# Stick-breaking attention in a four-layer trunk: the two newest key blocks' softplus values added once on VectorE, so that one matmul sums both

## The chip, the cores and the metric

The program runs on one core of a Trainium2 chip. The metric is the device time of one execution in microseconds; below 2% (some 57 us here) a difference counts as no difference in the verdicts.

## What is computed

A trunk of four layers is evaluated for 512 prompt frames and 64 sample frames, with D = 1024. Layers 0 and 3 mix with stick-breaking attention (16 heads of 64), layer 1 with a short gated convolution, layer 2 with gated linear attention; a squared-ReLU MLP follows each. Only the attention is touched:

```python
def stick_breaking_block(q, k, v, q_pos, k_pos):
    z = einsum('bqhd,bkhd->bhqk', q, k) * (SB_HEAD_DIM ** -0.5)
    mask = k_pos[None, :] < q_pos[:, None]
    log_not = where(mask, log_sigmoid(-z), 0.0)
    rev = cumsum(log_not, axis=3, reverse=True)
    tail = pad(rev[..., 1:], ...)
    a = where(mask, exp(log_sigmoid(z) + tail), 0.0)
    return einsum('bhqk,bkhd->bqhd', a, v)
```

So the weight of a key needs, beside its own score, the sum of softplus(z) = -log_sigmoid(-z) over all keys that are newer than it. The prompt's queries attend to the prompt's keys, the 64 sample queries to 256 cached keys and their own 64.

## The kernel before

Everything lies in SBUF: activations X as 8 blocks of 128 rows by 576 tokens (512 prompt, 64 sample). Dense layers run in slabs of 256 weight columns. SyncE loads a slab into `raw[:, s % 2]`; ScalarE rounds it to a high part `whi` (L766), VectorE makes the low part `wlo` (L1096); TensorE multiplies with three products for each 128x128 block (L384: high by high, high by low, low by high), always in two halves of 288 tokens. That is most of the time. The order on every engine is the order in which the code is written; the engines meet only in counting semaphores.

The attention of a layer is eight head pairs (`PAIRS`), each of three units, so 24 units u. A unit is one block of 128 key rows against all queries that see it, for both heads e = 0, 1. `b = 2 - u % 3`:

- u % 3 == 0 (b = 2), 448 columns: key block 2 against query blocks 2 and 3 (columns 0 to 255), key block 3 against query block 3 (256 to 383), the sample's own 64 keys (384 to 447).
- u % 3 == 1 (b = 1), 512 columns: key block 1 against query blocks 1 to 3 (0 to 383), cached keys 0 to 127 (384 to 447) and 128 to 255 (448 to 511) against the sample.
- u % 3 == 2 (b = 0), 512 columns: key block 0 against all four query blocks.

For a unit, `scores` (L441, L448) puts masked scores into one of three PSUM pairs `zduo[u % 3]`. ScalarE takes Exp (L867) and Ln (L872) of them into `weighted(u)`; VectorE's `softplus` clamps the result (L1201), rounds it to a high part (L1205, signals `sp_hi`) and subtracts for the low part (L1207, signals `sp_lo`), both in `parts(u)`. Then `cumulative(u)` on TensorE (L474, signals `r_ready`) adds the sums over newer keys to the scores in PSUM: for each part and each e, a triangular matmul over the unit's own columns and then matmuls with a matrix of minus ones, one for each newer key block and query range. ScalarE's `weights(u)` (L877, signals `a_ready`) takes Exp of the total over `weighted(u)`, and `weighted_values(u)` (L505) multiplies by the values. `scores(u)` waits for `weights(u - 3)`, since they use the same PSUM pair.

TensorE's order in the steady loop is `scores(k + 2)`, `cumulative(k)`, `weighted_values(k - 1)`; ScalarE's is `weights(k - 1)`, `logs(k + 1)`, `exponents(k + 2)`; VectorE runs `softplus(u)` one after the other, with `output` after u % 3 == 1. The first units are woven into a head in which cached keys and values are transposed on TensorE (L526, L534) and copied out by VectorE (L1175) and ScalarE (L840).

`split_r` is the same memory as the `raw` slabs: its upper half (`raw[:, 1]`) serves as `parts(u)` for u % 4 == 3. SyncE loads the output projection's slab 1 into it once three units from the last are summed (`r_ready`, `units - 3`). The lower half, `raw[:, 0]`, takes slab 2 directly behind it.

Of the kernel before, what the change touches and what calls it, by code (L numbers as in the profile page):

```python
# [82 lines left out]
def trunk(nc, x_prompt, x_sample, cache_sb_k, cache_sb_v, state_conv, state_gla, norm_mix, norm_mlp, sb_w_qkv, sb_w_o,  # L83
          conv_w_in, conv_w, conv_w_out, gla_w_in, gla_w_gk2, gla_b_gk, gla_norm, gla_w_o, mlp_w_up, mlp_w_down,
          norm_final, y_prompt, y_sample, sb_k_p, sb_v_p, sb_k_s, sb_v_s, conv_p, conv_s, gla_p, gla_s):
    with ExitStack() as ctx:
# [76 lines left out]
        ck_in, cv_in = sem("ck_in"), sem("cv_in")  # L163
        z_ready, e_ready, l_ready, sp_ready = (sem(n) for n in ("z_ready", "e_ready", "l_ready", "sp_ready"))
        sp_hi, sp_lo, r_ready, a_ready, av_done = (sem(n) for n in ("sp_hi", "sp_lo", "r_ready", "a_ready", "av_done"))
        sbt_ready, sbt_v, sbt_a = sem("sbt_ready"), sem("sbt_v"), sem("sbt_a")

        u_ready, y_ready, g_ready, conv_pre = sem("u_ready"), sem("y_ready"), sem("g_ready"), sem("conv_pre")
# [53 lines left out]
        def parts(u):  # L222
# [9 lines left out]
                return [v.rearrange("p (e c) -> p e c", e=2) for v in (hi, lo)]  # L232
            return [both[:, i * D:(i + 1) * D].rearrange("p (e c) -> p e c", e=2) for i in range(2)]

        zduo = [duo[i][:, :].rearrange("p (e c) -> p e c", e=2) for i in range(3)]
        obank, osbank = bank[6], bank[7]

# [81 lines left out]
        @block.sync  # L319
        def _(sp):  # L320
            for t in range(NT):
                src = x_prompt[0, t * P:(t + 1) * P, :] if t < 4 else x_sample[0]
                n = P if t < 4 else TS
                sp.dma_start(flat(0, 9)[0:n, t * D:(t + 1) * D], src).then_inc(x_in[t], 16)

            def load(base, w, count, units=None):
                def body(s, u):
                    sp.wait_ge(w_lo, base + s + 1)
                    if units is not None and isinstance(s, int) and s == 1:
                        sp.wait_ge(r_ready, units - 3)  # L330
                    sp.dma_start(raw[:, u], w[:, :, bass.ds(s * SLAB, SLAB)]).then_inc(slab_in[u], 16)
                slabs(sp, count, body, 0 if units is None else 2)

            for layer in range(4):
                base = first_slab(layer)
                if layer == 2:
                    for i, of in enumerate((0, 2 * D, D)):
                        load(base + OUT_SLABS * i, mix_in[layer][:, :, of:of + D], OUT_SLABS)
                elif layer == 1:
                    for s in range(IN_SLABS):  # L340
                        col = P * in_chunk(layer, s, 0)
                        sp.wait_ge(w_lo, base + s + 1)
                        sp.dma_start(raw[:, s % 2], mix_in[layer][:, :, col:col + SLAB]).then_inc(slab_in[s % 2], 16)
                else:
                    load(base, mix_in[layer], IN_SLABS)
                load(base + IN_SLABS, mix_out[layer], OUT_SLABS, UNITS * (layer // 3 + 1) if layer in (0, 3) else None)
                for g in range(GROUPS):
                    b = base + IN_SLABS + OUT_SLABS + 2 * OUT_SLABS * g
                    load(b, cols(mlp_w_up[layer][:, g * D:(g + 1) * D]), OUT_SLABS)
                    load(b + OUT_SLABS, cols(mlp_w_down[layer][g * D:(g + 1) * D, :]), OUT_SLABS)  # L350


            for t in range(NT):
                dst, n = (y_prompt[0, t * P:(t + 1) * P, :], P) if t < 4 else (y_sample[0], TS)
                sp.wait_ge(y_v, t + 2)
                sp.wait_ge(y_a, t + 1)
                sp.dma_start(dst, VT[0:n, t, :]).then_inc(y_stored, 16)
            sp.wait_ge(y_stored, 16 * NT)
            sp.wait_ge(kv_stored, 16 * 8)
            sp.wait_ge(stored, 16 * STORES)  # L360
# [3 lines left out]
        def _(pe):  # L364
# [64 lines left out]
            def stick_breaking(layer, sb_index):  # L429
# [36 lines left out]

                def cumulative(u):

                    b, z = 2 - u % 3, zduo[u % 3]
                    for part, ready in ((0, sp_hi), (1, sp_lo)):  # L470
                        pe.wait_ge(ready, first + u + 1)
                        for e in range(2):
                            def acc(which, lo, hi, back, of):
                                return pe.matmul(z[:, e, lo:hi], sums[:, which, :], parts(u - back)[part][:, e, of:of + hi - lo],  # L474
                                                 start=False, stop=False, skip_group_check=True)
                            mm = acc(0, 0, WIDE[u % 3], 0, 0)
                            if b == 2:
                                mm = acc(1, 128, 256, 0, 256)
                            elif b == 1:
                                acc(1, 128, 384, 1, 0)  # L480
                                acc(1, 256, 384, 1, 256)
                                acc(1, 384, 448, 1, 384)
                                acc(1, 448, 512, 1, 384)
                                mm = acc(1, 384, 448, 0, 448)
                            elif b == 0:
                                acc(1, 128, 512, 1, 0)
                                acc(1, 256, 512, 2, 0)
                                mm = acc(1, 384, 512, 2, 256)
                    mm.then_inc(r_ready, 1)

                def weighted_values(u):
# [267 lines left out]
        def _(act):  # L759
# [97 lines left out]
            def stick_breaking(layer, sb_index):  # L857
                first = UNITS * sb_index

                def exponents(u):  # L860
                    if u == 0 and sb_index:
                        act.wait_ge(kv_stored, 16 * 4 * sb_index)
                    if u >= 5:
                        act.wait_ge(av_done, first + u - 4)
                    act.wait_ge(z_ready, first + u + 1)
                    w = WIDE[u % 3]
                    act.activation(weighted(u)[:, :, 0:w], zduo[u % 3][:, :, 0:w], ACT.Exp).then_inc(e_ready, 1)  # L867

                def logs(u):
                    e = weighted(u)[:, :, 0:WIDE[u % 3]]  # L870
                    act.wait_ge(e_ready, first + u + 1)
                    act.activation(e, e, ACT.Ln, bias=1.0).then_inc(l_ready, 1)  # L872

                def weights(u):
                    w = WIDE[u % 3]
                    act.wait_ge(r_ready, first + u + 1)
                    act.activation(weighted(u)[:, :, 0:w], zduo[u % 3][:, :, 0:w], ACT.Exp).then_inc(a_ready, 1)  # L877

                def output(p):
                    act.wait_ge(av_done, first + 3 * p + 3)  # L880
                    act.activation(hhi[:, p, 0:TP], obank[:, :], ACT.Copy)
                    act.activation(hhi[:, p, TP:T], osbank[:, 0:TS], ACT.Copy).then_inc(mix_hi, 1)

                def cached_keys(n):
                    sb_evacuate(sb_index, n, CKT[:, 2 * n:2 * n + 2, :].rearrange("p c k -> p (c k)"), bank[7][:, :])

                exponents(0)
                cached_keys(1)
                logs(0)
                exponents(1)  # L890
                cached_keys(3)
                logs(1)
                values(sb_index, 5)
                exponents(2)
                values(sb_index, 7)
                weights(0)
                values(sb_index, 9)
                logs(2)
                values(sb_index, 11)
                values(sb_index, 13)  # L900
                exponents(3)
                for k in range(2, UNITS + 1):
                    weights(k - 1)
                    if k % 3 == 1:
                        output((k - 4) // 3)
                    if k + 1 < UNITS:
                        logs(k + 1)
                    if k + 2 < UNITS:
                        exponents(k + 2)
                output(PAIRS - 1)  # L910
# [178 lines left out]
        def _(dve):  # L1089
# [102 lines left out]
            def stick_breaking(layer, sb_index):  # L1192
                first = UNITS * sb_index

                def softplus(u):

                    w = WIDE[u % 3]
                    s = weighted(u)[:, :, 0:w]
                    hi, lo = (t[:, :, 0:w] for t in parts(u))
                    dve.wait_ge(l_ready, first + u + 1)  # L1200
                    dve.scalar_tensor_tensor(s, s, LN_MAX, zduo[u % 3][:, :, 0:w], ALU.min, ALU.max).then_inc(sp_ready, 1)  # L1201
                    dve.wait_ge(sp_ready, first + u + 1)
                    if u >= 4:
                        dve.wait_ge(r_ready, first + last_sum(u - 4) + 1)
                    dve.tensor_copy(hi, s).then_inc(sp_hi, 1)  # L1205
                    dve.wait_ge(sp_hi, first + u + 1)
                    dve.tensor_tensor(lo, s, hi.bitcast(F32), ALU.subtract).then_inc(sp_lo, 1)  # L1207

                def output(p):
                    dve.wait_ge(mix_hi, 8 * layer + p + 1)  # L1210
# [556 lines left out]
```

## Time and profile before

| | us |
|---|---|
| runs | 2845.40, 2875.87, 2877.62 |
| median of the runs | 2875.87 |
| profiled execution, own time | 2865.92 |
| its span | 2864.2 |
| TensorE busy in it | 2822.2 (99%) |
| VectorE busy | 1257.0 (44%) |
| ScalarE busy | 862.1 (30%) |
| mean granted TensorE clock | 0.993 of full |

The span is the profiled part of an execution; its own time is 1.7 us more. A busy share tells how long an engine had something in flight, not that it was at its peak: a matmul's row lasts longer than the distance to the next one's start. The attention of layer 0 stands from about 175 to 307 us, that of layer 3 from about 2250 to 2382 us.

### The profile page before, as it was taken

How to read it: one execution, taken by the hardware profiler on the slowest of the kernel's cores; microseconds unless marked ns; L12 is line 12 of the kernel's file. 1: busy time of each engine (PE TensorE's matmuls, PEld its weight loads, DVE VectorE, ACT ScalarE, POOL GpSimd, SP SyncE). 2: the span in 40 equal slices, each digit the busy share in tenths (PEclk: the TensorE clock that was granted, in tenths of full speed). 3: DMA queues.
4: the chain of work that ended last, by engine and by line, in shares of the span. 5: the costliest groups of instructions: out<-in, count | busy, mean ns of one | idle time of the engine just before them, and what ended most of it. 6: DMA issues, size and time to landing. Idle time of an engine off the chain costs nothing.

```text
span 2864.2 us, 49238 instructions
## 1 busy us (share of the span) xinstructions
PE 2822.2 (99%) x21138; PEld 2740.5 (96%) x21138; DVE 1257.0 (44%) x1641; ACT 862.1 (30%) x945; POOL 220.5 (8%) x223
## 2 busy tenths in 40 slices
PE   8999999999999999999999999999999999999998
PEld 8987999999999999999999899999999879999998
DVE  4346443333455433334377543333433464433333
ACT  3136432222311322223233432221321364322222
POOL 3000100000111200000132110000000001000001
PEclk9999999999999999999999999999999999999999
DMA  4210232222222222222211122222232102322221
GB/s 153 80 56 1 82 115 84 78 89 74 89 76 86 76 90 86 88 88 74 74 60 59 53 74 88 89 74 89 74 103 88 48 1 89 107 88 76 87 78 58
DMA packets 205499, 223.45 MB, mean 78 GB/s; under 512 B 3751, under 2 KB 200465, under 8 KB 205361
## 3 DMA queue, kind: packets, MB, share of 16 engines
q1 hardware_dynamic: 200992, 206.06, 22.2%
q0 software_dynamic: 4368, 15.38, 1.5%
q8 instruction: 107, 1.75, 0.3%
q14 instruction: 32, 0.25, 0.0%
HBM read 208.56 MB, written 12.86 MB: 77 GB/s over the span
## 4 chain that ended last, share of the span: by engine, by line
PE 96%; ACT 2%; DVE 1%; issue 0%; DMA 0%; ACTq 0%; DVEq 0%
PE bank L384 86%; PE bank L474 4%; PE bank L448 2%; PE bank L616 1%; ACT big L877 1%; PE bank L505 1%; PE bank L441 1%; PE bank L670 0%; PE bank L653 0%; PE bank L568 0%; PE bank L401 0%; PE bank L669 0%; DVE mixs L1175 0%; DVE wlo L1096 0%; PE bank L581 0%; PE bank L534 0%
## 5 line engine op out<-in xcount | busy, mean ns | idle before, releaser
L384 PE MATMUL bank<-ahi,whi 128*128 128x288 f32 x3584 | 771.9, 297 | 6.6 <-DVE alo L1121 6.6
L384 PE MATMUL bank<-alo,whi 128*128 128x288 f32 x3584 | 768.1, 296 | 0.0
L384 PE MATMUL bank<-ahi,wlo 128*128 128x288 f32 x3584 | 767.9, 296 | 0.0
L766 ACT ACTIVATE whi<-raw 128x2048 fp32r<-128x2048 f32 x191 | 364.5, 1908 | 831.1 <-PE bank L384 831.1
L384 PEld LDWEIGHTS bank<-ahi,whi 128*128 128x128 f32 x3584 | 579.2, 189 | 8.7 <-DVE wlo L1096 6.8
L384 PEld LDWEIGHTS bank<-ahi,wlo 128*128 128x128 f32 x3584 | 578.9, 189 | 0.0
L384 PEld LDWEIGHTS bank<-alo,whi 128*128 128x128 f32 x3584 | 578.8, 189 | 0.0
L384 PE MATMUL bank<-hhi,whi 128*128 128x288 f32 x2560 | 549.2, 296 | 1.6 <-DVE hlo L1444 1.6
L384 PE MATMUL bank<-hhi,wlo 128*128 128x288 f32 x2560 | 547.4, 295 | 0.0
L384 PE MATMUL bank<-hlo,whi 128*128 128x288 f32 x2560 | 547.2, 295 | 0.0
L1096 DVE TENSOR_TENSOR wlo<-raw,whi 128x2048 fp32r<-128x2048 f32 x192 | 442.1, 2303 | 202.3 <-ACT whi L766 199.5
L384 PEld LDWEIGHTS bank<-hhi,whi 128*128 128x128 f32 x2560 | 412.1, 189 | 3.5 <-issue 3.4
L384 PEld LDWEIGHTS bank<-hhi,wlo 128*128 128x128 f32 x2560 | 412.4, 189 | 0.0
L384 PEld LDWEIGHTS bank<-hlo,whi 128*128 128x128 f32 x2560 | 412.3, 189 | 0.0
L1488 DVE TENSOR_TENSOR X<-bank,X 128x288 f32 (+1 forms) x320 | 131.3, 452 | 488.4 <-PE bank L384 487.9
L1058 ACT ACTIVATE big<-big 128x576 f32<-128x576 f32 x128 | 87.8, 686 | 542.6 <-DVE big L1505 542.6
L1505 DVE SCALAR_TENSOR_TENSOR big<-bank,rstd 128x288 f32<-128x288 f32 x256 | 105.1, 452 | 226.3 <-PE bank L384 226.2
L1509 DVE TENSOR_TENSOR hlo<-big,hhi 128x576 f32 (+1 forms) x128 | 97.1, 758 | 183.1 <-ACT hhi L1059 183.1
L1169 DVE TENSOR_TENSOR big<-bank,rstd 128x288 f32<-128x288 f32 x152 | 62.4, 452 | 206.8 <-PE bank L384 206.5
L1583 POOL MEMSET big<- 128x576 f32 x8 | 4.6, 579 | 1704.6 <-PE bank L384 1704.6
L797 ACT ACTIVATE ahi<-X,vec (+1 forms) x64 | 49.0, 775 | 244.9 <-DVE X L1488 244.8
L1587 POOL TENSOR_TENSOR big<-big 128x576 f32<-128x576 f32 x63 | 97.8, 1552 | 289.9 <-ACT big L800 289.9
(260 smaller groups left out, 1691.8 us busy)
## 6 DMA issues: line engine op xcount, KB each, us to landing
raw<-in_mlp_w_up SPq DMA_DIRECT2D x64, 1024.0 KB, 5.3
raw<-in_mlp_w_down SPq DMA_DIRECT2D x64, 1024.0 KB, 4.9
raw<-in_sb_w_qkv SPq DMA_DIRECT2D x24, 1024.0 KB, 5.1
raw<-in_conv_w_in SPq DMA_DIRECT2D x12, 1024.0 KB, 5.1
raw<-in_gla_w_in SPq DMA_DIRECT2D x12, 1024.0 KB, 5.3
raw<-in_sb_w_o SPq DMA_DIRECT2D x8, 1024.0 KB, 5.1
out<-mixs POOLq DMA_DIRECT2D x2, 2048.0 KB, 7.7
out<-big POOLq DMA_DIRECT2D x2, 2048.0 KB, 8.3
```

The source lines that it names most:

```text
L384: mm = pe.matmul(acc[h][:, 0:HALF], w[:, u, k, m * P:(m + 1) * P], a[:, k, h * HALF:(h + 1) * HALF], start=(k == 0 and w is whi and a is a ...
L448: mm = pe.matmul(z[0:k.shape[1], e, lo:hi], k, big[r, p, q_lo:q_lo + hi - lo], start=False, stop=False, skip_group_check=True)
L474: return pe.matmul(z[:, e, lo:hi], sums[:, which, :], parts(u - back)[part][:, e, of:of + hi - lo], start=False, stop=False, skip_group_ch ...
L766: act.activation(whi[:, 1 - u], raw[:, 1 - u], ACT.Copy).then_inc(w_hi, 1)
L797: act.activation(at(ahi, j), at(X, j), ACT.Copy, scale=g).then_inc(xg_hi, 1)
L1058: act.activation(sq_h[m], relu_t[m], ACT.Square).then_inc(hid_sq, 1)
L1096: dve.tensor_tensor(wlo[:, u], raw[:, u], whi[:, u].bitcast(F32), ALU.subtract).then_inc(w_lo, 1)
L1169: ins = dve.tensor_tensor(dst, acc, rstd[:, hs], ALU.mult)
L1488: ins = dve.tensor_tensor(part(X, j, hs), bank[2 * m + h][:, 0:HALF], part(X, j, hs), ALU.add)
L1505: ins = dve.scalar_tensor_tensor(relu_t[m][:, hs], bank[2 * m + h][:, 0:HALF], 0.0, rstd[:, hs], ALU.max, ALU.mult)
L1509: dve.tensor_tensor(at(hlo, c), sq_h[m], at(hhi, c).bitcast(F32), ALU.subtract).then_inc(hid_ready, 1)
L1587: pool.tensor_tensor(ssq, ssq, sq_x, ALU.add).then_inc(ssq_add, 1)
```

## The change

In `cumulative`, three sets of matmuls are merged; each set is issued for both parts and both e. The prompt columns of u % 3 == 1 and 2 that need key block 3 beside key block 2 (two matmuls each before) take one matmul over `newer`, which holds block 2's values for query block 2 and, for query block 3, the sum of the values of blocks 2 and 3. The sample's own values, which two matmuls of 64 columns added to both cached halves, are read twice by one matmul of 128 columns through an operand that is repeated. `newer_sum` and `newer` are made on VectorE by the new `newer_keys`, right behind `softplus(u)` of u % 3 == 0; they lie in `raw[:, 0]`, whose slab 2 SyncE now loads after the layer's last `cumulative`.

```diff
+        nw_sum, nw_hi, nw_lo = sem("nw_sum"), sem("nw_hi"), sem("nw_lo")
...
+        newer_sum = raw[:, 0].rearrange("p k c -> p (k c)")[:, D:D + 2 * P].rearrange("p (e c) -> p e c", e=2)
+        newer = [split_r[:, 512 * i:512 * i + 512].rearrange("p (e c) -> p e c", e=2) for i in range(2)]
...
-                    if units is not None and isinstance(s, int) and s == 1:
-                        sp.wait_ge(r_ready, units - 3)
+                    if units is not None and s in (1, 2):
+                        sp.wait_ge(r_ready, units - 3 if s == 1 else units)
...
-                            mm = acc(0, 0, WIDE[u % 3], 0, 0)
+                            own = parts(u)[part][:, e, :]
+                            mm = acc(0, 0, WIDE[u % 3], own[:, 0:WIDE[u % 3]])
                             if b == 2:
-                                mm = acc(1, 128, 256, 0, 256)
-                            elif b == 1:
-                                acc(1, 128, 384, 1, 0)
-                                acc(1, 256, 384, 1, 256)
-                                acc(1, 384, 448, 1, 384)
-                                acc(1, 448, 512, 1, 384)
-                                mm = acc(1, 384, 448, 0, 448)
-                            elif b == 0:
-                                acc(1, 128, 512, 1, 0)
-                                acc(1, 256, 512, 2, 0)
-                                mm = acc(1, 384, 512, 2, 256)
+                                mm = acc(1, 128, 256, own[:, 256:384])
+                                continue
+                            if e == 0:
+                                pe.wait_ge((nw_hi, nw_lo)[part], 2 * pair + 2)
+                            if b == 1:
+                                acc(1, 128, 384, newer[part][:, e, :])
+                                new = parts(u - 1)[part][:, e, 384:448]
+                                acc(1, 384, 512, new.unsqueeze(1).to_broadcast([P, 2, TS]))
+                                mm = acc(1, 384, 448, own[:, 448:512])
+                            else:
+                                acc(1, 128, 512, parts(u - 1)[part][:, e, 0:384])
+                                mm = acc(1, 256, 512, newer[part][:, e, :])
...
                     act.wait_ge(r_ready, first + u + 1)
+                    if u % 3 == 0:
+                        act.wait_ge(nw_hi, 2 * (PAIRS * sb_index + u // 3) + 1)
+                        act.wait_ge(nw_lo, 2 * (PAIRS * sb_index + u // 3) + 1)
...
+                    if u % 3 == 0:
+                        newer_keys(u, s)
+
+                def newer_keys(u, s):
+
+                    pair, near, far = PAIRS * sb_index + u // 3, slice(0, P), slice(P, 2 * P)
+                    dve.tensor_tensor(newer_sum, s[:, :, far], s[:, :, 256:384], ALU.add).then_inc(nw_sum, 1)
+                    if u:
+                        dve.wait_ge(r_ready, first + u)
+                    dve.tensor_copy(newer[0][:, :, near], s[:, :, near]).then_inc(nw_hi, 1)
+                    dve.wait_ge(nw_hi, 2 * pair + 1)
+                    dve.tensor_tensor(newer[1][:, :, near], s[:, :, near], newer[0][:, :, near].bitcast(F32),
+                                      ALU.subtract).then_inc(nw_lo, 1)
+                    dve.wait_ge(nw_sum, pair + 1)
+                    dve.tensor_copy(newer[0][:, :, far], newer_sum).then_inc(nw_hi, 1)
+                    dve.wait_ge(nw_hi, 2 * pair + 2)
+                    dve.tensor_tensor(newer[1][:, :, far], newer_sum, newer[0][:, :, far].bitcast(F32),
+                                      ALU.subtract).then_inc(nw_lo, 1)
```

TensorE's instructions of one `cumulative` part for one e, in the second head pair of layer 0 (`bank<-split_r,sums` and `bank<-whi,sums` are products of the sums' matrices with softplus parts that lie in those buffers). Before, first u % 3 == 1, then u % 3 == 2:

```order
L474 MATMUL bank<-whi,sums 128x512
L474 MATMUL bank<-split_r,sums 128x256
L474 MATMUL bank<-split_r,sums 128x128
L474 MATMUL bank<-split_r,sums 128x64 x2
L474 MATMUL bank<-whi,sums 128x64
...
L474 MATMUL bank<-whi,sums 128x512
L474 MATMUL bank<-whi,sums 128x384
L474 MATMUL bank<-split_r,sums 128x256
L474 MATMUL bank<-split_r,sums 128x128
```

And of the change, at the same place:

```order
L477 MATMUL bank<-whi,sums 128x512
L477 MATMUL bank<-split_r,sums 128x256
L477 MATMUL bank<-split_r,sums 128x128
L477 MATMUL bank<-whi,sums 128x64
...
L477 MATMUL bank<-whi,sums 128x512
L477 MATMUL bank<-whi,sums 128x384
L477 MATMUL bank<-split_r,sums 128x256
```

Six matmuls became four and four became three; the 128 columns that are left in the first group are the repeated operand.

VectorE in the second head pair of layer 0, from `softplus(3)` on, with the semaphores that an instruction waits for; first before, then the change:

```order
L1201 SCALAR_TENSOR_TENSOR big<-big,bank 128x2x448 [waits l_ready]
L1205 CAST split_r<-big 128x2x448 [waits sp_ready]
L1207 TENSOR_TENSOR split_r<-big,split_r 128x2x448 [waits sp_hi]
L1201 SCALAR_TENSOR_TENSOR e<-e,bank 128x1024 [waits l_ready]
```

```order
L1209 SCALAR_TENSOR_TENSOR big<-big,bank 128x2x448 [waits l_ready]
L1213 CAST split_r<-big 128x2x448 [waits sp_ready]
L1215 TENSOR_TENSOR split_r<-big,split_r 128x2x448 [waits sp_hi]
L1222 TENSOR_TENSOR raw<-big 128x256
L1225 CAST split_r<-big 128x2x128 [waits r_ready]
L1227 TENSOR_TENSOR split_r<-big,split_r 128x2x128 [waits nw_hi]
L1230 CAST split_r<-raw 128x2x128 [waits nw_sum]
L1232 TENSOR_TENSOR split_r<-raw,split_r 128x2x128 [waits nw_hi]
L1209 SCALAR_TENSOR_TENSOR e<-e,bank 128x1024 [waits l_ready]
```

Five instructions stand between two softplus steps, the second of them behind a wait for the `cumulative` of the unit before.

## Rows read from the trace of the kernel before

**Rows 1.** The page's chain that ended last, shares of the span by engine.

```profile
PE 96%; ACT 2%; DVE 1%; issue 0%; DMA 0%; ACTq 0%; DVEq 0%
```

**Rows 2.** The chain of waits, one head pair: start us, us, what.

```profile
253.90 3.32 PE bank L474 x24
...
257.24 1.03 ACT big L877
...
259.84 2.71 PE bank L474 x16
...
265.00 1.39 PE bank L474 x8
...
268.96 3.32 PE bank L474 x24
```

**Rows 3.** TensorE's timeline: start us, us, engine, line, operation, operands, count.

```profile
168.27 0.43 PE L384 MATMUL bank<-alo,whi 128*128 128x288 f32 x2
168.54 0.42 PE L384 MATMUL bank<-ahi,wlo 128*128 128x288 f32 x2
...
245.39 0.45 PE L474 MATMUL bank<-split_r,sums 128*128 128x512 f32 x1
...
246.03 0.45 PE L474 MATMUL bank<-split_r,sums 128*128 128x512 f32 x1
...
253.83 1.78 PE L474 MATMUL bank<-whi,sums 128*128 128x512 f32 x12
255.44 1.76 PE L474 MATMUL bank<-wlo,sums 128*128 128x512 f32 x12
```

**Rows 4.** VectorE's groups with shapes kept apart: count, busy us, mean ns, idle before.

```profile
L1207 DVE TENSOR_TENSOR wlo<-big,whi 128x1024 fp32r<-128x1024 f32 x12 | 14.7, 1225 | 0.4
L1205 DVE CAST whi<-big 128x1024 fp32r<-128x1024 f32 x12 | 8.3, 694 | 0.4
L1126 DVE TENSOR_TENSOR big<-rstd 128x576 f32<-128x576 f32 x8 | 6.1, 764 | 11.8 <-ACT rstd L807 11.8
```

**Rows 5.** VectorE's timeline in the same pair; in brackets idle time before.

```profile
253.73 0.21 DVE L1212 TENSOR_TENSOR hlo<-bank,hhi 128x64 fp32r<-128x64 f32 x1
...
260.26 0.63 DVE L1205 CAST split_r<-big 128x896 fp32r<-128x896 f32 x1
260.92 1.09 DVE L1207 TENSOR_TENSOR split_r<-big,split_r 128x896 fp32r<-128x896 f32 x1
264.57 1.22 DVE L1201 SCALAR_TENSOR_TENSOR big<-big,bank 128x1024 f32<-128x1024 f32 x1 [2.56 <-ACT big L872]
```

**Rows 6.** The chain of waits at the attention's head, layers 0 and 3.

```profile
182.45 0.61 DVE mixs L1175
...
2257.26 0.61 DVE mixs L1175
```

**Rows 7.** Busy time by engine in the head of layer 0; granted clock behind POOL.

```profile
174.00:193.00 19.00, 14.39 (x115) 10.83 (x115) 11.80 (x16) 10.48 (x14) 0.73 (x1) 1.00 0.16 56
```

**Rows 8.** The chain of waits at the end of layer 0's attention.

```profile
297.53 3.31 PE bank L474 x24
300.84 1.06 PE bank L505 x12
301.90 2.70 PE bank L474 x16
```

**Rows 9.** VectorE's timeline there, the last softplus.

```profile
300.52 0.69 DVE L1205 CAST split_q<-big 128x1024 fp32r<-128x1024 f32 x1
301.25 1.23 DVE L1207 TENSOR_TENSOR split_q<-big,split_q 128x1024 fp32r<-128x1024 f32 x1
```

**Rows 10.** The page's DMA issues: count, KB each, median us to landing.

```profile
raw<-in_sb_w_o SPq DMA_DIRECT2D x8, 1024.0 KB, 5.1
```

**Rows 11.** ScalarE's timeline, the rounding of the output projection's slab 2.

```profile
322.87 1.90 ACT L766 ACTIVATE whi<-raw 128x2048 fp32r<-128x2048 f32 x1
```

**Rows 12.** Busy time and granted clock in layer 2, as Rows 7.

```profile
1626.00:1636.00 10.00, 6.97 (x32) 6.81 (x33) 6.81 (x12) 6.13 (x14) 0.00 (x0) 0.50 0.01 2
```

More of the change, by code:

```diff
@@ L328, in body @@
                     sp.wait_ge(w_lo, base + s + 1)
-                    if units is not None and isinstance(s, int) and s == 1:
-                        sp.wait_ge(r_ready, units - 3)
+                    if units is not None and s in (1, 2):
+                        sp.wait_ge(r_ready, units - 3 if s == 1 else units)
                     sp.dma_start(raw[:, u], w[:, :, bass.ds(s * SLAB, SLAB)]).then_inc(slab_in[u], 16)
-                slabs(sp, count, body, 0 if units is None else 2)
+                slabs(sp, count, body, 0 if units is None else count)
             for layer in range(4):
@@ L467, in cumulative @@
                 def cumulative(u):
-                    b, z = 2 - u % 3, zduo[u % 3]
+                    b, z, pair = 2 - u % 3, zduo[u % 3], PAIRS * sb_index + u // 3
                     for part, ready in ((0, sp_hi), (1, sp_lo)):
@@ L472, in cumulative, with acc @@
                         for e in range(2):
-                            def acc(which, lo, hi, back, of):
-                                return pe.matmul(z[:, e, lo:hi], sums[:, which, :], parts(u - back)[part][:, e, of:of + hi - lo],
-                                                 start=False, stop=False, skip_group_check=True)
-                            mm = acc(0, 0, WIDE[u % 3], 0, 0)
-                            if b == 2:
-                                mm = acc(1, 128, 256, 0, 256)
-                            elif b == 1:
-                                acc(1, 128, 384, 1, 0)
-                                acc(1, 256, 384, 1, 256)
-                                acc(1, 384, 448, 1, 384)
-                                acc(1, 448, 512, 1, 384)
-                                mm = acc(1, 384, 448, 0, 448)
-                            elif b == 0:
-                                acc(1, 128, 512, 1, 0)
-                                acc(1, 256, 512, 2, 0)
-                                mm = acc(1, 384, 512, 2, 256)
+                            def acc(which, lo, hi, src):
+                                return pe.matmul(z[:, e, lo:hi], sums[:, which, :], src, start=False, stop=False,
+                                                 skip_group_check=True)
+                            own = parts(u)[part][:, e, :]
+                            mm = acc(0, 0, WIDE[u % 3], own[:, 0:WIDE[u % 3]])
+                            if b == 2:
+                                mm = acc(1, 128, 256, own[:, 256:384])
[10 more added lines that the diff above has]
+                                mm = acc(1, 256, 512, newer[part][:, e, :])
                     mm.then_inc(r_ready, 1)
```

## The prediction

> **What bounds the kernel now.** I read the page's chain first: 96% of it is TensorE, 2% ScalarE, 1% VectorE [rows 1], so what shortens TensorE's own work shortens the end, and only there. The second view is that chain inside an attention. One head pair takes 268.96 - 253.90 = 15.06 us [rows 2]. In it each `cumulative` stands in full: 3.32 us for u % 3 == 1, 2.71 us for u % 3 == 2, 1.39 us for u % 3 == 0. Behind the first two stands `weights` of ScalarE, 1.03 us [rows 2], for which the next scores wait. VectorE is not in the loop's chain. The third view, TensorE's timeline, gives the price of a matmul as the distance between starts, since its own row is longer (0.43 us for a pair whose successor starts 0.27 us on) [rows 3]. The last are VectorE's timeline beside it, the head, where VectorE is in the chain [rows 6], and the end [rows 8, 9].
>
> **What the change takes away.** For each part and e it removes two matmuls of u % 3 == 1 and one of u % 3 == 2: 12 in a head pair, 192 in 16 pairs. A pair of 288-column matmuls takes 0.27 us, so one takes 0.133, of which the columns are 120 ns at the full clock, 2.4 GHz (2.4 columns a ns), and 13 ns come on top [rows 3]. By that a 512-column matmul takes 0.227 us, one of 384 0.173, one of 256 0.120. The group of u % 3 == 2 (512, 384, 256, 128) takes 246.03 - 245.39 = 0.64 us [rows 3], which leaves 0.64 - 0.52 = 0.12 for the one of 128 columns. Two groups of u % 3 == 1 (512, 256, 128 and three of 64) take 255.44 - 253.83 = 1.61 us [rows 3], 0.805 each, which leaves 0.458 for four small ones, 0.115 each. So a small matmul costs a fixed 0.115 us however few columns it has, and merging gains by the instruction, not by the column. 12 x 0.115 = 1.38 us a pair, 22.1 us in 16 pairs. A repeated operand is in no row; I take it at 0.115 like another 128-column matmul. Its bounds are nothing lost and double the price: 4 of them in 16 pairs, 7.4 us, kept for the range.
>
> That fixed price is where a rule speaks against the change. The Trainium skill, "TensorE: Matmul & The Clock Gate", section "Back-to-back issue gap", gives an isolated warm matmul N / 2.4 + 2.5 ns, from which I estimate 29 ns for 64 columns and 56 for 128: 0.46 us a pair, 7.3 us in all. For a stream of weight loads and matmuls it names about 81 ns at 128 columns, an estimated 15.6 us in all. Its section on LDWEIGHTS gives columns over 1.2, an estimated 107 ns for 128, and every matmul here loads its weights anew; the rows' 0.115 stands near that figure and above both others.
>
> **What it adds.** Five VectorE instructions a pair, each of 256 elements a partition. Tensor-tensor takes 1.225 us for 1024 and 0.764 for 576 [rows 4], 1.03 ns an element, so 0.435 for 256. A copy takes 0.694 for 1024 [rows 4] and 0.63 for 896 [rows 5], 0.5 ns an element, so 0.31. Three and two of them are 1.92 us, say 1.9 with the gaps, of which 0.43 (the sum) stands ahead of the wait. Bounds, from the shortest and the longest row: 5 x 0.21 = 1.1 [rows 5] and 5 x 1.22 = 6.1 [rows 4].
>
> In the loop this is hidden. `softplus` of u % 3 == 0 ends at 262.01 and the next one starts at 264.57, after 2.56 us idle [rows 5]. The wait for the `cumulative` before (its end is 259.84 + 2.71 = 262.55 [rows 2]; less what is cut from it) holds little: sum to 262.4, the other 1.5 to about 264.1. If the cover were gone, the next softplus would be late: its high part is ready at 264.57 + 1.22 + 0.04 + 0.69 = 266.5, wanted at 268.96 [rows 2, 4, 5], so another 2.4 us are spare. The wait that `weights` of u % 3 == 0 now has ends near 263.3; its `cumulative` ends at 265.00 + 1.39 = 266.4 [rows 2], later anyway. `newer` is asked for at about 269.3. Behind the five instructions on VectorE only softplus and, one unit on, `output` are queued.
>
> In the **head** it is not hidden. Behind `softplus(0)` the copy of the cached keys stands in the chain in both layers [rows 6], and now waits for the five: 1.9 us each, 3.8 us. Bounds: nothing, if other waits there swallow it, and 12.2.
>
> At the **end** no scores are left, and TensorE comes to the last `cumulative` sooner than its input. It starts at 301.90 now; with 0.92 taken from the one before [rows 8] it would want to start at 300.98, but the high part ends at 301.21 [rows 9], 0.23 us late, and the low part (302.48) is a little late too, after a first half of now 1.12 us. I take 0.35 a layer, 0.7 in all; bounds nothing and 1.8.
>
> SyncE's load of slab 2 is moved behind the last `cumulative`, to 304.6 [rows 8]. It lands about 5.1 us later [rows 10], near 310; ScalarE rounds it at 322.87 [rows 11]. It costs nothing: TensorE's work on slab 0 covers it with 12 us to spare. Slab 3, queued behind it on SyncE, waits for slab 1's split near 311.7 in any case.
>
> **The sum** is -22.1 + 3.8 + 0.7 = -17.6 us against the profiled execution's 2865.9, or 2848.3. The median of the runs is 10 us above that execution, and from there it is 2858.3. The three runs spread from 2845.4 to 2877.6, more than the effect. I take the middle of the two, 2853 (that is 2870.9 before), and take the rivals' nets from 2870.9 too.
>
> **The rivals.**
> - *Small matmuls cost their columns.* If the spacing of what remains fills the freed slots, the gain is that of the columns alone: 4 x 256 in a pair, at 0.133 us for 288 [rows 3] 0.47 us, 7.6 in all, net -3.1: about 2868. Against it stand both groups of rows 3. Chance 4%. The skill's isolated gap, above, would give nearly the same.
> - *The clock.* In layer 2 a stretch of 10 us, in which TensorE was busy 6.97, ran at granted 0.50, which is 1.2 GHz [rows 12]; where TensorE has work, 10 us of this lose 5. In the attention's head it was busy 14.39 of 19 us at 1.00 [rows 7], and now idles 1.9 us longer. If the clock fell in both heads, 10 us go: net -7.6, about 2863. Chance 6%. The same page, section "HAM oscillation", says that waits between stretches of matmuls make the gate throttle again; rows 7 show none.
> - *VectorE becomes the bound, slower than before.* The five are small, strided, and wait for one another. Place: the softplus of u % 3 == 1. From 262.0 to the high part's need the loop covers 2.56 + 2.4 = 4.9 us, so the five bind once they take 4.9 us instead of 1.9, and with the heads the whole is slower from 5.5 us on ((22.1 - 0.7 + 16 x 4.9) / 18); at the 6.1 us bound a pair loses 1.2, leaving 0.2 x 16 = 3 us of gain against 12.2 us of heads and 1.8 at the ends: net +11, about 2882. For it: no strided 256-element row. Against it: the 64-element row of 0.21 us [rows 5] shows no large fixed cost. Chance 3%.
> - *The repeated operand is read slowly.* At double price its 64 matmuls give back 7.4 us: net -10.2, about 2861. No row has such an operand; a 64-column matmul that reads one plain block shows no more than the fixed price. Chance 9%.
>
> The forecast has 78%; beside it the runs' own spread matters more than any rival. The range starts at the fastest run less the full gain, 2845.4 - 22 = 2823, taken as 2825, and ends at 2868, which holds the first, second and fourth rival and the slowest run less 10 us. A measurement of this kernel can tell about 2% (57 us) from no change; no case reaches that. Within 2%: 97%, faster 2%, slower 1%, both for what I have not seen.
>
> **What would show it.** In the changed chain: `cumulative` x16 at 2.40 us in place of x24 at 3.32, x12 at 2.23 in place of x16 at 2.71, a pair in 13.7 us; in the head 1.9 us of VectorE ahead of the copy; five VectorE rows of about 0.43 and 0.31; no idle of TensorE or ScalarE that ends on them in the loop; no clock below 1.00 from 175 to 300 us. Wrong would be a repeated-operand matmul with more than 0.12 us to its successor, a loop whose chain runs through VectorE, or a slab 2 that ScalarE waits for.

## The result, and the profile after

| | before | the change |
|---|---|---|
| median of 20 runs each, us | 2867.53 | 2853.03 |
| lowest to highest | 2845.40 to 2877.77 | 2833.57 to 2860.51 |
| profiled execution, span | 2864.2 | 2854.4 |
| attention of layer 0, of layer 3 | 131.23, 131.23 | 123.12, 123.12 |

The ratio is 0.9936, with a 95% interval of 0.9919 to 0.9952: about 18 us less, between 14 and 23 (the two medians alone differ by 14.5), a gain clear of the noise and below the 2% of the verdicts. The forecast was 2853, with 97% for a change within 2%. The last line is the finer measure and is used below: from the first masked scores to the output projection's first product, read from TensorE's timeline. It repeats within 0.1 us where nothing acts on it (131.23 in both layers). For the change it reads 299.41 - 176.29 = 123.12 in layer 0, so 8.11 us went in each layer, 16.2 in both.

TensorE's timeline of the changed kernel, first and last row of that stretch:

```profile
176.29 0.45 PE L444 MATMUL bank<-maskb,identb 128*128 128x128 bf16 x4 [0.92 <-DVE big L1177]
...
299.41 0.53 PE L387 MATMUL bank<-hhi,whi 128*128 128x288 f32 x2
```

The chain of waits in one pair, the answer to [rows 2]; the same steps in the same order, the two merged ones shorter:

```profile
251.20 2.43 PE bank L477 x16
...
253.65 1.03 ACT big L885
...
256.25 2.30 PE bank L477 x12
...
261.00 1.40 PE bank L477 x8
...
264.98 2.43 PE bank L477 x16
```

A pair takes 264.98 - 251.20 = 13.78 us, where it took 15.06. The `cumulative` of u % 3 == 1 went from 3.32 to 2.43, that of u % 3 == 2 from 2.71 to 2.30. VectorE stands in no step of it. Its timeline beside it shows why: behind the fifth new instruction it still waits half a microsecond for ScalarE.

```profile
259.34 0.29 DVE L1230 CAST split_r<-raw 128x256 fp32r<-128x256 f32 x1
259.66 0.43 DVE L1232 TENSOR_TENSOR split_r<-raw,split_r 128x256 fp32r<-128x256 f32 x1
260.58 1.22 DVE L1209 SCALAR_TENSOR_TENSOR big<-big,bank 128x1024 f32<-128x1024 f32 x1 [0.50 <-ACT big L877]
```

The chain in layer 0's head, where [rows 6] had the copy right behind the first softplus:

```profile
183.25 0.33 DVE raw L1222
183.59 0.21 DVE split_r L1225
...
183.83 0.42 DVE split_r L1227
184.25 0.22 DVE split_r L1230
...
184.49 0.42 DVE split_r L1232
184.91 0.61 DVE mixs L1183
```

The five take 184.91 - 183.25 = 1.66 us of the chain. And one thing is new there, the clock (busy time by engine, then the granted clock behind POOL, as in [rows 7]):

```profile
187.00:190.00 3.00, 2.99 (x13) 2.79 (x14) 2.93 (x4) 1.81 (x3) 0.00 (x0) 0.50 0.00 0
```

TensorE had idled 2.52 us for the late copy (before, 0.86 at this place):

```profile
185.57 1.09 PE L539 MATMUL bank<-ident,big 128*128 128x128 f32 x8 [2.52 <-DVE mixs L1183]
```

It then ran 3.4 us at half clock, 1.2 GHz; in layer 3's head the same. In this execution that cost nothing: from the copy of the cached keys to the `cumulative` of unit 1 the chain takes 196.08 - 184.91 = 11.17 us, before 193.62 - 182.45 = 11.17.

The chain at the end of layer 0's attention, the answer to [rows 8, 9]:

```profile
289.96 1.03 PE bank L510 x4
...
291.01 0.60 ACT hhi L889
...
291.73 0.96 ACT big L877
...
292.71 1.23 DVE big L1209
...
293.96 0.70 DVE split_q L1213
...
294.71 2.59 PE bank L477 x12
```

The `cumulative` of unit 22 has left the chain; the last softplus has entered it, through ScalarE's output copy and logarithm, and the last `cumulative` takes 2.59 us where its shape takes 2.30. TensorE's timeline has the two waits, for the high part ahead of it and, at the weight load (PEld) in its middle, for the low part:

```profile
294.71 0.67 PE L477 MATMUL bank<-split_q,sums 128*128 128x512 f32 x2 [0.27 <-DVE split_q L1213]
...
295.97 0.30 PEld L477 LDWEIGHTS bank<-split_q,sums 128*128 128x128 f32 x2 [0.21 <-DVE split_q L1215]
```

### The profile page after: what moved, and what is told of

The parts are those of the page before. It is cut to its first block, busy times and chain, and to the rows that moved or that the text cites. A ratio compares the mean times of both kernels' runs of the same rounds, so it can differ in the third digit from the quotient of the medians.

```text
span 2854.4 us, 48946 instructions
## 1 busy us (share of the span) xinstructions
PE 2811.0 (98%) x20946; PEld 2726.8 (96%) x20946; DVE 1283.1 (45%) x1721; ACT 862.5 (30%) x945; POOL 220.6 (8%) x223
## 4 chain that ended last, share of the span: by engine, by line
PE 96%; ACT 2%; DVE 1%; issue 0%; DMA 0%; ACTq 0%; DVEq 0%
PE bank L387 86%; PE bank L477 3%; PE bank L451 2%; PE bank L621 1%; ACT big L885 1%; PE bank L510 1%; PE bank L444 1%; PE bank L675 0%; PE bank L658 0%; PE bank L573 0%; PE bank L539 0%; PE bank L404 0%; PE bank L674 0%; DVE wlo L1104 0%; PE bank L586 0%; ACT e L885 0%
```

## The experiments

Each ran with a profile; those with a ratio were also timed in five rounds against the kernel before on the same chip. The attention is read as above, in one profiled execution of each.

| kernel | attention, layers 0 and 3, us | one pair | ratio to before, 95% |
|---|---|---|---|
| before | 131.23, 131.23 | 15.06 | |
| the change | 123.12, 123.12 | 13.78 | 0.9936 [0.9919, 0.9952] |
| 1 repeated operand alone | 127.69, 127.69 | 14.61 | 0.9981 [0.9959, 1.0004] |
| 2 newer keys alone | 126.32, 126.30 | 14.23 | 1.0004 [0.9981, 1.0028] |
| 3 VectorE's work and waits alone | 132.98, 133.43 | 15.08 | |
| 4 one matmul narrowed | 130.94, 130.94 | 15.03 | |
| 5 four more on VectorE | 123.57, 124.00 | 13.78 | |
| 6 eight more on VectorE | 132.51, 132.50 | 14.97 | |
| 7 the moved load alone | 131.31, 131.31 | | |
| 8 first pair on GpSimd | 121.89, 121.89 | 13.79 | 0.9934 [0.9911, 0.9956] |
| 9 newer widened | 121.41, 120.42 | 13.57 | 0.9925 [0.9898, 0.9952] |
| 10 two matmuls | 119.49, 119.72 | 13.18 | 0.9882 [0.9856, 0.9908] |
| 11 two matmuls, head in order | 117.84, 117.81 | 13.20 | 0.9899 [0.9874, 0.9924] |
| 12 the change again | 123.15, 124.01 | 13.78 | 0.9920 [0.9892, 0.9949] |

### What a small matmul costs

**Experiment 1.** The kernel before with the repeated operand, on a line of its own:

```diff
-                                acc(1, 384, 448, 1, 384)
-                                acc(1, 448, 512, 1, 384)
+                                new = parts(u - 1)[part][:, e, 384:448]
+                                pe.matmul(z[:, e, 384:512], sums[:, 1, :], new.unsqueeze(1).to_broadcast([P, 2, TS]),
+                                          start=False, stop=False, skip_group_check=True)
```

> The kernel before with the repeated operand alone: the sample's own values go to both cached halves by one matmul of 128 columns instead of two of 64, for each part and e. The columns stay the same, 64 matmuls go (4 in each of 16 head pairs). Fixed price (a small matmul costs about 0.11 us whatever its columns): 0.45 us a pair, each layer's attention 131.2 to about 127.6 us, the whole about 7 us less. Column price: no change, 131.2. Repeated operand read at double price: no change or worse, 131.2 or more.

A layer's attention became 3.54 us shorter with not one column less. The chain gives the repeated operand its own step (L483):

```profile
253.69 0.61 PE bank L474 x3
254.30 0.11 PE bank L483
254.41 0.57 PE bank L474 x4
254.98 0.12 PE bank L483
```

0.11 to 0.12 us: the price of any small matmul. The column price (no gain) and the slow operand (no gain or a loss) are both refuted. The timed ratio can't tell 7 us from nothing; the profile's attention can.

**Experiment 4.** The kernel before, one matmul narrowed, so that it leaves out some of the sums:

```diff
-                                mm = acc(1, 384, 512, 2, 256)
+                                mm = acc(1, 448, 512, 2, 320)
```

> The kernel before, with the last matmul of u % 3 == 2 cut from 128 columns to 64 (it leaves out the sums of key block 3 for half of query block 3). The number of matmuls stays, 256 columns go in a pair. Fixed price: no change, attention 131.2 us, the cumulative x16 still 2.71 us. Column price: 0.12 us a pair, 0.95 a layer, 130.3 us.

```profile
255.71 3.32 PE bank L474 x24
...
261.65 2.66 PE bank L474 x16
```

In its chain the narrowed `cumulative` takes 2.66 us where it took 2.71: 256 columns fewer save 0.05, not the 0.12 of the column price, and 0.29 a layer, not 0.95. Experiment 1 and this one hold the two apart, and both say: the instruction costs; the columns of a small one cost a third of the column price (0.29 of 0.95), not quite the nothing that was expected.

**Experiment 2.** The change with the repeated operand taken back:

```diff
-                                acc(1, 384, 512, new.unsqueeze(1).to_broadcast([P, 2, TS]))
+                                acc(1, 384, 448, new)
+                                acc(1, 448, 512, new)
```

> The change without the repeated operand: VectorE makes the newer sums, 8 matmuls go in each pair, the sample's values again take two matmuls of 64 columns. Fixed price: 8 x 0.11 = 0.88 us a pair, 7.0 a layer, less 1.65 for the head and some 0.3 at the end: attention about 126.1 us, the whole about 10 us less than before. Column price (256 columns in 4 groups at 0.46 ns): 0.47 a pair, 3.8 a layer, attention about 129.3. The sum of this gain and the first kernel's should be the change's 8.1 us a layer within 0.5, if the two halves don't act on each other.

```profile
250.43 2.88 PE bank L477 x20
...
255.93 2.30 PE bank L477 x12
```

126.3 us in both layers, 4.92 less than before; 4.92 + 3.54 = 8.46 against the change's 8.11, so the halves add up within 0.35. What is lost is at the end: here the last `cumulative` takes 2.41 us, 0.11 over its shape, and with both halves it comes earlier still and loses more. The timed ratio shows no gain (1.0004), and its interval leaves room for 5.4 us at most, though the profile shows 9.8 us in both layers. So something outside the attention took time in those runs; the section on the hardware has a candidate, which the profile of one execution can't prove.

One more thing is in this profile: in layer 0 TensorE had the same stall as in the change, and the clock did not fall:

```profile
182.99 1.09 PE L540 MATMUL bank<-ident,big 128*128 128x128 f32 x8 [2.53 <-DVE mixs L1184]
```

```profile
183.00:190.00 7.00, 4.86 (x36) 4.12 (x37) 5.02 (x6) 3.66 (x6) 0.00 (x0) 1.00 0.00 1
```

In layer 3 it fell for 3.4 us. The two attentions took 126.32 and 126.30 us: there the low clock cost nothing.

### What VectorE's work costs

**Experiment 3.** The change, with TensorE's matmuls as before (`new` is the sample's own values); the waits stay:

```diff
-                                acc(1, 128, 384, newer[part][:, e, :])
+                                acc(1, 128, 384, parts(u - 1)[part][:, e, 0:256])
+                                acc(1, 256, 384, parts(u - 1)[part][:, e, 256:384])
...
-                                acc(1, 384, 512, new.unsqueeze(1).to_broadcast([P, 2, TS]))
+                                acc(1, 384, 448, new)
+                                acc(1, 448, 512, new)
...
-                                mm = acc(1, 256, 512, newer[part][:, e, :])
+                                acc(1, 256, 512, parts(u - 2)[part][:, e, 0:256])
+                                mm = acc(1, 384, 512, parts(u - 2)[part][:, e, 256:384])
```

> The change's VectorE work and all its waits, but TensorE's matmuls as before, none merged. If VectorE is hidden in the loop and shows in the head alone: attention 131.23 + 1.65 = 132.9 us in both layers, pairs still 15.06 us. If the five instructions or their waits cost something in the loop: above 133.5, with VectorE or ScalarE waits in the chain of a pair. If the fall of the clock in the head comes of the longer stall, it is here too.

Layer 0 took 1.75 us more than before, of which 1.66 are the head's, and its pairs took 15.08 where it was 15.06: hidden in the loop, bare in the head. Layer 3 took another 0.45 more. The chain there shows four transposes at 1.13 us; at the full clock such a step takes 0.67.

```profile
2268.06 0.61 DVE mixs L1186
...
2268.72 1.13 PE bank L542 x4
```

So the clock fell in both heads here too, with TensorE's work untouched: the longer stall goes before it. Over all profiles of this case: in 14 heads TensorE's longest wait was 2.5 to 2.7 us and the clock fell in 13 of them, layer 0 of experiment 2 being the exception; in 12 heads it was at most 1.45 us and the clock fell in none; in experiment 9 it was 1.86 us in both layers and the clock fell in layer 0 alone. What the fall costs depends on where in the chain it lands.

**Experiments 5 and 6.** The change with n = 4 and n = 8 more instructions:

```diff
+                    if u:
+                        for i in range(n):
+                            ...
+                            dve.tensor_tensor(spare, newer_sum, newer_sum, ALU.subtract).then_inc(nw_more, 1)
```

> The change with four more VectorE instructions of 256 elements (0.42 us each, written to unused memory) behind the five, in every head pair but the first of a layer. In the changed kernel VectorE is idle 2.7 us in a pair of 13.78 (11.1 busy), and the high part of the softplus that comes next lies 2.4 us ahead of TensorE's need. Both readings say 1.7 us more is hidden: attention 123.1 us, up to 0.5 more at the end of it.

> The same with eight more, 3.4 us a pair. By the one stretch that the prediction reckoned with (0.5 us idle and 2.4 us lead behind the five, 2.9 in all) a pair loses 0.5 us: attention about 126.5 us. By VectorE's work in the whole pair (11.1 + 3.4 = 14.5 us against 13.78, with the gaps that it can't close more) a pair becomes 14.7 us or longer: attention 130 us or more, and VectorE and ScalarE stand in the chain of each pair.

VectorE's row for a pair of the changed kernel says 11.50 us busy, not the 11.1 that I had added up, so 2.3 us were free. Four were hidden, up to 0.45 us at the end of layer 0. Layer 3 has 0.9: in its head the low clock also fell on four transposes of the chain, which took 1.13 us in place of 0.67. Eight made the pair 14.97 us and the attention 132.5, longer than before the change. The chain of waits names VectorE in every step; its first and last row here are one pair apart:

```profile
253.67 1.22 DVE big L1210
...
268.64 1.22 DVE big L1210
```

and VectorE's row (third busy time) is full but for half a microsecond:

```profile
253.67:268.64 14.97, 13.81 (x102) 9.43 (x102) 14.45 (x26) 9.35 (x13) 0.00 (x0) 1.00 0.00 1
```

The local reading, idle time and lead behind the five, would have let 2.9 us more pass and asked for 0.5 a pair; the reading of the whole pair (work plus 0.5) was right. The prediction's rival had the right mechanism and the wrong place of its edge: it put it at 4.9 us for the group. The group of experiment 6 takes 1.66 + 3.64 = 5.3 us and a pair is 1.19 longer than the change's, so by this estimate the room ran out at about 4.1.

**Experiment 7.** The kernel before, with the change's SyncE lines alone (the wait for `r_ready` in front of slab 2).

> The kernel before with the moved load alone: slab 2 of the output projection is loaded behind the layer's last cumulative. If its 12 us of cover hold, nothing changes: attention 131.2 us and no wait of ScalarE for a DMA behind it. If the load is on the path, TensorE waits in the output projection, up to 5 us a layer.

131.31 against 131.23: nothing. In the changed kernel ScalarE rounds slab 2 16.15 us behind the attention's end (315.56 - 299.41), before 16.16 (322.87 - 306.71).

**Experiment 8.** The change, the first pair's five instructions in GpSimd's program, in front of its stores:

```diff
-                    if u % 3 == 0:
+                    if u % 3 == 0 and u:
                         newer_keys(u, s)
...
+                pool.wait_ge(sp_ready, UNITS * sb_index + 1)
+                pool.tensor_tensor(newer_sum, s[:, :, far], s[:, :, 256:384], ALU.add).then_inc(nw_sum, 1)
+                ...
```

> The change, with the five instructions of each layer's first head pair on GpSimd, which is idle there, instead of VectorE. If the head's cost is only VectorE's time ahead of the copies: attention 123.12 - 1.65 = about 121.5 us in both layers, no fall of the clock in the head, and the whole about 3 us less than the change. If GpSimd is too slow (its 576-element additions take 1.55 us, so the five may take 4 us) ScalarE's weights of the first unit wait for it, and half of the gain is lost; if the clock's fall has another cause, it stays.

The clock stayed at 1.00 in both heads, and 1.23 us of the 1.66 came back.

```profile
187.00:190.00 3.00, 1.52 (x12) 1.05 (x10) 2.25 (x3) 0.92 (x1) 0.00 (x0) 1.00 0.01 3
```

The missing 0.4 is in one row of VectorE, 1.50 us for a subtraction that takes 1.09 otherwise; GpSimd's two rows beside it are long as well:

```profile
181.56 1.50 DVE L1215 TENSOR_TENSOR wlo<-stg,whi 128x896 fp32r<-128x896 f32 x1
```

```profile
180.96 1.16 POOL L1648 TENSOR_TENSOR raw<-stg 128x256 f32<-128x256 f32 x1 [4.89 <-DVE stg L1209]
182.07 1.25 POOL L1649 CAST split_r<-stg 128x256 fp32r<-128x256 f32 x1
183.40 0.73 POOL L1651 TENSOR_TENSOR split_r<-stg,split_r 128x256 fp32r<-128x256 f32 x1
```

GpSimd's tensor-tensor rows take 0.73 us while VectorE copies out of PSUM or waits, and 1.16 here, beside VectorE's rounding and subtraction. The Trainium skill, "SBUF — State Buffer", section "Who interferes with whom", says that the two share a pair of SBUF ports under an exclusive lock, and that a VectorE tensor-tensor with both inputs in SBUF meets GpSimd's reads there; these rows agree.

### How far it goes

**Experiment 9.** `newer` widened to 384 columns a head; GpSimd copies the sample's own values twice behind the key blocks, and starts the first pair's work a step later than in experiment 8:

```diff
-                                acc(1, 128, 384, newer[part][:, e, :])
-                                new = parts(u - 1)[part][:, e, 384:448]
-                                acc(1, 384, 512, new.unsqueeze(1).to_broadcast([P, 2, TS]))
...
+                                acc(1, 128, 512, newer[part][:, e, :])
                                 mm = acc(1, 384, 448, own[:, 448:512])
```

> The change, further: newer is widened to 384 columns by the sample's own values, copied twice behind the two key blocks by GpSimd, so that u % 3 == 1 takes three matmuls (512, 384, 64) where the change takes four (512, 256, 128, 64); the first pair's newer keys are on GpSimd, and start only when VectorE's softplus(0) is done. By the prices (a matmul of 128 columns at 0.115 goes, one of 256 at 0.120 becomes one of 384 at 0.173) 0.06 us a group, 0.25 a pair, 2.0 a layer: attention 121.9 - 2.0 = 119.9 us. By the number alone (0.11 for each that goes) 0.45 a pair: 118.3. If VectorE's subtraction in the head was slowed by GpSimd's work beside it, it takes 1.09 us again and the head gives 0.4 more.

The step takes 2.21 us in place of 2.43, a pair 0.21 less: as the prices said (0.25), far from 0.45, since a 384-column matmul is no small one. The attention did not reach 119.9. GpSimd's later start freed the subtraction of softplus(0) (1.09 us again) but moved its work under softplus(1), where a subtraction took 1.64 us in place of 1.23, so the head won nothing. And in layer 0 the clock fell and cost 1.0 us (121.41 against 120.42 in layer 3, where it stayed at 1.00).

**Experiment 10.** The newer cached block's values are added to the sample's own as well:

```diff
-                                acc(1, 128, 512, newer[part][:, e, :])
-                                mm = acc(1, 384, 448, own[:, 448:512])
...
+                                mm = acc(1, 128, 512, newer[part][:, e, :])
```

with, on VectorE, behind the softplus of u % 3 == 1,

```diff
+                        dve.tensor_tensor(cached_sum, cached_sum, s[:, :, 448:512], ALU.add).then_inc(cs_sum, 1)
...
+                        dve.tensor_copy(newer[0][:, :, c], cached_sum).then_inc(cs_hi, 1)
...
+                        dve.tensor_tensor(newer[1][:, :, c], cached_sum, newer[0][:, :, c].bitcast(F32), ...)
```

> The same, and the newer cached block's values are added to the sample's own on VectorE, so that u % 3 == 1 takes two matmuls (512, 384). Three VectorE instructions of 128 elements (about 0.29, 0.22 and 0.29 us) are added behind the softplus of u % 3 == 1, 0.8 us a pair; GpSimd makes three small copies. TensorE: 4 x (0.607 - 0.43) = 0.71 us a pair off, 5.7 a layer: attention about 116 us if VectorE stays off the chain. VectorE is then busy about 11.9 of 13.1 us; by the run with eight more instructions its pair can't be shorter than its work plus 0.5 us, so it should just fit. If the latency behind the softplus of u % 3 == 1 counts instead, or GpSimd slows VectorE, VectorE stands in the chain and the attention stays at 119 us or more.

```profile
251.95 1.83 PE bank L480 x8
...
265.13 1.83 PE bank L480 x8
```

A pair takes 13.18 us and VectorE is still off its chain, with 12.13 us of work in it. The attention stayed at 119.5, where 116 was expected, mostly for the head's sake: softplus(1) slowed by GpSimd (a rounding took 1.19 us in place of 0.69), three more instructions ahead of a copy, and a clock that fell again while the remaining transposes ran.

**Experiment 11.** The same with the head in order; GpSimd also copies the first pair's sample values last, and VectorE's three instructions for unit 1 stand only where the edit shows them:

```diff
                 values(sb_index, 8)
+                cached_keys_sum(1, weighted(1))
                 values(sb_index, 10)
...
-                pool.wait_ge(sp_lo, UNITS * sb_index + 1)
+                pool.wait_ge(sp_ready, UNITS * sb_index + 1)
```

> The kernel with two matmuls for u % 3 == 1, its head put in order: GpSimd starts the first pair's newer keys at once behind the clamp of softplus(0), and VectorE's three instructions for unit 1 stand behind a copy of values, where it waits 0.75 us for TensorE's transposes. If the head lost 2.0 us to these and to the clock that fell behind the longer stall: head as with GpSimd alone, no clock below 1.00 in the attention, pairs still 13.18 us, attention 119.5 - 1.6 = about 117.9 us in both layers. If the loss was the three instructions' alone: 118.8 and the clock falls again.

The three instructions fit into VectorE's wait for transposes, the clock stayed up, and the attention is 117.8 us: 13.4 a layer less than before and 5.3 less than the change. At the layer's end some 1.2 us of what the pairs gained is still lost, since the `cumulative` of unit 22 waits for these instructions and the last softplus stands behind them. (An estimate: from the start of that `cumulative` to the attention's end it is 293.38 - 284.79 = 8.59 us, before 306.71 - 297.46 = 9.25, of which the shorter steps should have taken 1.9.)

**Experiment 12.** The change as it is, on the same chip.

> The change itself once more, beside the kernel above on the same chip: attention 123.12 us in both layers, the clock falls in both heads, and the whole about 16 us less than before.

The medians of experiments 11 and 12 on one chip are 2839.17 and 2846.85, before 2866.50; the intervals of the two ratios overlap (0.9899 [0.9874, 0.9924] and 0.9920 [0.9892, 0.9949]), so that experiment 11 beats the change is shown by the attention's rows, not by the timed runs. Nor do these rank experiment 10 (0.9882, on another chip) against 11. The change's second profile has 123.15 us in layer 0 as expected, but in layer 3's head a longer stretch at half clock, 6.8 us, for which it pays 0.9 us:

```profile
2246.09 3.82 PE bank L539 x16
2249.90 2.24 PE bank L477 x8
2252.14 0.61 PE bank L539 x4
```

## Why the prediction was right, by its steps

- **What bounds it.** TensorE's own work in the loop; right. Both halves came out of the chain one for one.
- **The gain of a pair.** Forecast 1.38 us, measured 1.28 (0.89 from u % 3 == 1, forecast 0.92; 0.41 from u % 3 == 2, forecast 0.48). The mechanism, a fixed price for each small matmul, is shown by experiments 1 and 4. The size was a little high: 0.115 us for each where 0.11 and 0.10 went. The estimate from the isolated gap of the Trainium skill, "TensorE: Matmul & The Clock Gate", section "Back-to-back issue gap" (7.3 us in all), is far off, and so is the 15.6 from its figure for a stream: 16 x 1.28 = 20.5 were measured. Its section "LDWEIGHTS (loading the stationary operand)", by which I estimated 107 ns for 128 columns, is the near one; that loading the weights is what sets the price, no run shows.
- **The repeated operand.** Taken at the price of any other; shown by experiment 1.
- **The five on VectorE.** Forecast 1.9 us, measured 1.66: the copies took 0.29 us where 0.31 was reckoned, and where one instruction need not wait for the last it starts before that one's row ends (0.34 us behind its start, for a row of 0.42). Hidden in the loop: right (experiment 3).
- **The head.** Forecast 3.8 us in both layers, measured 3.3.
- **The end.** Forecast 0.35 a layer. 8 pairs x 1.29 = 10.3 less the head's 1.65 less the 8.11 measured leaves 0.55. The high part was late about as reckoned (0.27 us of idle time, 0.23 reckoned); the term was too small in the wait for the low part, put at "a little", which cost 0.29 (2.59 in place of 2.30). VectorE's own timing did not move: the last high part is ready 3.75 us behind the start of the `cumulative` of unit 22 in both kernels. Experiment 5 shows that the term grows when VectorE gets more.
- **The moved load.** Nothing; right (experiment 7).
- **The clock.** The rival came true in its mechanism and hardly in its price. The clock fell in both heads behind the longer stall, for 3.4 us where 10 were reckoned, and mostly beside VectorE's work: it cost 0 in one profile, 0.9 in one head of another. The sign "no clock below 1.00" failed, and with it the reading that rows 7 show no danger; the stall does not bring the fall every time (experiment 2, layer 0).
- **The sum.** -17.6 forecast, -16.2 in the attention's rows, -18 by the ratio, -14.5 by the medians. That the median came out at 2853.0 is in part luck: the level before was taken halfway between two, at 2870.9, and 20 runs then put it at 2867.5.

## What to carry to other kernels

Price TensorE's work by the distance between starts and fit it with two numbers, one for the column and one for the instruction. For the small ones here (64 and 128 columns at 0.10 to 0.12 us) merging paid by the instruction, beyond 256 columns the columns counted in full (experiment 9), and a repeated operand merged for nothing. When work is moved to an engine that is off the chain, ask for its room in the whole period, not behind the one place where it is put. And look apart at the first round of a loop: there the engine that is idle later may be the bound, and a gap that it has in any case is the place for the new work.

## What the runs showed of the hardware

The runs spread from 2845 to 2878 us before the change, and the profiles show something of that size outside the attention. In some stretches of the dense layers a 288-column matmul follows the last at 0.130 us, in others at 0.133, at granted clock 1.00 in both. The same 50 us of the kernel before and of the change (count of TensorE's matmuls first):

```profile
1000.00:1050.00 50.00, 50.00 (x387) 50.00 (x386) 21.46 (x29) 14.90 (x16) 0.00 (x0) 1.00 0.29 95
```

```profile
1000.00:1050.00 50.00, 50.00 (x377) 50.00 (x376) 19.30 (x25) 13.30 (x14) 0.00 (x0) 1.00 0.27 85
```

Between the attentions the two profiles run the same program. By 1382 us of the kernel before, where the spacing had differed for some 400 us, the change's execution was 9.9 us behind. Layer 2 gave 4.6 of them back; there the granted clock was 0.50 for some 24 us before and 17 in the change. In sum the one of before took 1943.58 us and the change's 1948.91. Most of why the profiled spans differ by 9.8 us and not by 16.2 is in these 5.3 us. That the same thing hid experiment 2's gain in its timed runs is possible and not shown; its one profiled execution took 1949.8 us between the attentions. Which stretches run at which spacing changed from execution to execution; the cause stays open.
